# The opening of a decoder kernel: x normalised before its transposes, and even and odd modulation sums kept apart

## The reference

```python
def sandwich(x, fn, g_pre, g_post, shift, scale, gate, res_w):
    h = rms_norm(x, g_pre) * (1.0 + scale[:, None]) + shift[:, None]
    y = rms_norm(fn(h), g_post)
    return x + res_w * gate[:, None] * y
...
mod = cond @ ada_w[l] + ada_b[l]
sh1, sc1, gt1, sh2, sc2, gt2, sh3, sc3, gt3 = jnp.split(mod, N_MOD, axis=-1)
```

## Time and profile before

| | us |
|---|---|
| median of 3 runs | 1982.17 (1980.71 to 1982.24) |
| the profiled execution, its own time | 1987.39 |
| its span | 1985.6 |
| TensorE busy | 1886.3 |
| VectorE busy | 1412.9 |
| ScalarE busy | 838.1 |

### The profile page before, as it was taken

The page is one execution under the profiler, slowest core; times in us unless marked ns, Lnnn a source line. Parts: engine busy times, 40 slices in busy tenths (PEclk is TensorE's granted clock), DMA queues, the critical chain, the costliest instruction groups (busy, mean ns, idle before and its releaser), DMA issues.

```text
span 1985.6 us, 21419 instructions
## 1 busy us (share of the span) xinstructions
PE 1886.3 (95%) x8582; PEld 1546.5 (78%) x8582; DVE 1412.9 (71%) x1477; ACT 838.1 (42%) x1067; POOL 20.6 (1%) x25
## 2 busy tenths in 40 slices
PE   2779999999999998999999999999999999999997
PEld 2558888888888888777777787788888888888895
DVE  4987888888888887765765566666666665555556
ACT  2214434443444343374555534644344434443443
POOL 0000000000000000000000000000000000000000
PEclk6779999999999999999999999999999999999999
DMA  9888998999999998545333434566666655555551
GB/s 344 323 318 323 355 347 338 352 340 343 344 342 349 346 344 306 186 141 179 128 127 128 149 135 168 191 233 244 243 233 233 244 201 191 191 191 191 196 196 74
DMA packets 204002, 486.80 MB, mean 245 GB/s; under 512 B 7984, under 2 KB 20992, under 8 KB 188800
## 3 DMA queue, kind: packets, MB, share of 16 engines
q1 hardware_dynamic: 202816, 482.79, 67.1%
q10 hardware_dynamic: 992, 2.63, 0.4%
q0 software_dynamic: 96, 0.02, 0.0%
HBM read 483.31 MB, written 2.10 MB: 244 GB/s over the span
## 4 chain that ended last, share of the span: by engine, by line
PE 86%; DVE 6%; issue 2%; DMA 2%; ACT 1%; DVEq 0%; SPq 0%; POOLq 0%; POOL 0%; ACTq 0%
PE ps_u L1373 10%; PE ps_g L1373 10%; PE ps_u L1374 9%; PE ps_u L1375 9%; PE ps_g L1375 9%; PE ps_g L1374 9%; PE ps_t L1373 4%; PE ps_t L1374 4%; PE ps_t L1375 4%; PE ps_y L1373 4%; PE ps_y L1374 4%; PE ps_y L1375 4%; DVE arena L1136 3%; DMA ada_raw<-in_ada_w 2%; DVE w_lo L842 1%
## 5 line engine op out<-in xcount | busy, mean ns | idle before, releaser
L842 DVE TENSOR_TENSOR w_lo<-w_raw,w_hi 128x1024 fp32r<-128x1024 f32 (+1 forms) x632 | 753.1, 1200 | 458.4 <-ACT w_hi L505 457.2
L505 ACT ACTIVATE w_hi<-w_raw 128x1024 fp32r<-128x1024 f32 (+1 forms) x632 | 657.4, 1042 | 952.1 <-PE ps_u L1375 342.1
L1373 PE MATMUL ps_g<-w_hi,xT_hi 128*128 128x512 f32 (+1 forms) x880 | 347.1, 394 | 21.4 <-DVE w_lo L842 11.4
L1373 PE MATMUL ps_u<-w_hi,xT_hi 128*128 128x512 f32 (+2 forms) x880 | 348.0, 395 | 19.1 <-DVE w_lo L842 18.3
L1375 PE MATMUL ps_g<-w_hi,xT_lo 128*128 128x512 f32 (+1 forms) x880 | 341.8, 388 | 0.0
L1375 PE MATMUL ps_u<-w_hi,xT_lo 128*128 128x512 f32 (+2 forms) x880 | 341.8, 388 | 0.0
L1374 PE MATMUL ps_g<-w_lo,xT_hi 128*128 128x512 f32 (+1 forms) x880 | 341.6, 388 | 0.0
L1374 PE MATMUL ps_u<-w_lo,xT_hi 128*128 128x512 f32 (+2 forms) x880 | 341.5, 388 | 0.0
L866 DVE SCALAR_TENSOR_TENSOR arena<-ada_raw,cond,arena 128x2048 f32<-128x2048 f32 x108 | 253.6, 2348 | 32.7 <-DMA ada_raw<-in_ada_w 32.0
L1373 PEld LDWEIGHTS ps_g<-w_hi,xT_hi 128*128 128x128 f32 x880 | 166.3, 189 | 62.4 <-DVE w_lo L842 19.4
L1373 PEld LDWEIGHTS ps_u<-w_hi,xT_hi 128*128 128x128 f32 x880 | 167.1, 190 | 58.8 <-DVE w_lo L842 22.6
(11 more groups left out here) (239 smaller groups left out, 1542.5 us busy)
## 6 DMA issues: line engine op xcount, KB each, us to landing
w_raw<-in_ffn_w_in SPq DMA_DIRECT2D x160, 1024.0 KB, 4.9
ada_raw<-in_ada_w SPq DMA_DIRECT2D x128, 1024.0 KB, 7.2
w_raw<-in_ffn_w_out SPq DMA_DIRECT2D x80, 1024.0 KB, 5.1
w_raw<-in_mix_w_in SPq DMA_DIRECT2D x32, 1024.0 KB, 5.0
arena<-in_ada_w SPq DMA_DIRECT2D x16, 1024.0 KB, 10.2
w_raw<-in_mix_w_out SPq DMA_DIRECT2D x16, 1024.0 KB, 5.0
w_raw<-in_ffn_w_in SPq DMA_DIRECT2D x16, 768.0 KB, 4.6
w_raw<-in_ffn_w_out SPq DMA_DIRECT2D x8, 768.0 KB, 4.2
```

Of the source, the lines that this page charges most:

```text
L505: nc.scalar.activation(w_hi[:, u % 4, 0:n, 0:width], w_raw[:, s, 2 * hf:2 * hf + n, 0:width], ACT.Copy).then_inc(hi_done, 1)
L842: nc.vector.tensor_tensor(w_lo[:, u % 4, 0:n, 0:width], w_raw[:, s, 2 * hf:2 * hf + n, 0:width], w_hi[:, u % 4, 0:n, 0:width].bitcast(F32) ...
L1373: nc.tensor.matmul(o, a_hi[:, k, rows], w_hi[:, b, c, 0:width], start=start, stop=False)
```

## The change

- x is normalised before it is transposed. ScalarE takes the squares, GpSimd the power, and ScalarE multiplies x by 1/rms per token, into `yacc`. TensorE transposes that, 16 transposes for each token tile. The diagonal, the row `rbc`, `xt_scale` and the old `xt_hi` and `xt_lo` are gone. In a strip ScalarE applies scale and shift in one pass in place (two instructions of 256 columns for each pair of chunks) and rounds in a second (one of 512), and VectorE subtracts (one of 512).
- A tile of `ada_w` now holds two k-chunks of both modulations, loaded by two DMAs of 512 KB instead of one of 1 MB. VectorE handles both modulations with one instruction of 2 x 512 columns. Even k-chunks go into `acc`, odd ones into `junk`; there are 16 instructions in a strip. TensorE adds the two in PSUM: `first_sums` has 16 matmuls instead of eight.
- In strip s VectorE does the lo part of units 2 to 5, each followed by two tiles of strip s + 1, and then `strip_start(s + 1)`: it waits for the sums, forms the columns, makes units 0 and 1 of strip s + 1 and the xT rest of all four chunks. TensorE's order (units 0 to 3, sums, units 4 and 5) is as before. `first_xt_hi` stands behind unit 1 on ScalarE.
- c is loaded first and has its own transpose; 50 filler matmuls stand before the transposes of x and 40 before the first sums. Four small loads of constants move from ScalarE's queue to the end of the first SwiGLU on SyncE's, and the instruction on `sink` with them.

```diff
-ADA_PRE = 32
+STRIP_TILES = 8
+ADA_PRE = STRIPS * STRIP_TILES
 MODS_PRE = ((0, 1), (1, 2))
 
 
...
+def first_count(s, i):
+
+    return STRIP_TILES * s + i + 1
 
 
 def ada_total(mod):
...
         s_done, e_done, p_ready = sem("s_done"), sem("e_done"), sem("p_ready")
                 for i in range(LOOP):
                     hidden(i + 2, g0 + 5 + 3 * i, NB)
                 if f == 0:
+                    sp.dma_start(dist_a[:, :], consts[:, 128:512]).then_inc(const_landed, 16)
+                    sp.dma_start(dist_b[:, :], consts[:, 512:896]).then_inc(const_landed, 16)
+                    sp.dma_start(kvg[:, :], kvn_in[0:1, :].broadcast_to((P, KV_RANK))).then_inc(const_landed, 16)
+                    sp.dma_start(sink[:, :], sinks_in[0:1, :].broadcast_to((P, A_HEADS))).then_inc(const_landed, 16)
...
-            sp.dma_start(small_rows[4 * KD:6 * KD, :], ada_b[0, 0:2 * D].rearrange("(k p) -> k p", p=P)).then_inc(c_landed, 16)
-            sp.dma_start(small_rows[3 * KD:4 * KD, :], c_in[0].rearrange("(k p) -> k p", p=P)).then_inc(c_landed, 16)
+            sp.dma_start(mod_rows[:, :], c_in[0].rearrange("(k p) -> k p", p=P)).then_inc(cond_landed, 16)
             for n in range(3):
                 sp.dma_start(small_rows[n * KD:(n + 1) * KD, :], norm_g[0, 2 * n].rearrange("(k p) -> k p", p=P)).then_inc(c_landed, 16)
-            sp.dma_start(small_rows[6 * KD:8 * KD, :], ada_b[0, 3 * D:5 * D].rearrange("(k p) -> k p", p=P)).then_inc(c_landed, 16)
+            sp.dma_start(small_rows[3 * KD:5 * KD, :], ada_b[0, 0:2 * D].rearrange("(k p) -> k p", p=P)).then_inc(c_landed, 16)
+            sp.dma_start(small_rows[5 * KD:7 * KD, :], ada_b[0, 3 * D:5 * D].rearrange("(k p) -> k p", p=P)).then_inc(c_landed, 16)
             sp.dma_start(more_rows[:, :], ada_b[0, 6 * D:8 * D].rearrange("(k p) -> k p", p=P)).then_inc(c_landed, 16)
...
-                for a in range(8):
-                    kg, m = divmod(a, 2)
-                    count = 8 * s + a
-                    need(sp, ada_done, count - 3)
-                    sp.dma_start(first_slots[a % 4].rearrange("p (k n) -> p k n", n=NB),
-                                 ada_w[0].rearrange("(k p) n -> p k n", p=P)[:, 4 * kg:4 * kg + 4, m * D + s * NB:m * D + (s + 1) * NB]
-                                 ).then_inc(ada_landed[a % 4], 16)
+                for i in range(STRIP_TILES):
+                    before, j = (s, i - 4) if i >= 4 else (s - 1, i + 4)
+                    if before >= 0:
+                        sp.wait_ge(ada_done, first_count(before, j))
+                    for m in range(2):
+                        slot = first_slots[i % 4][:, m * 2 * NB:(m + 1) * 2 * NB].rearrange("p (k n) -> p k n", k=2)
+                        sp.dma_start(slot, ada_w[0].rearrange("(k p) n -> p k n", p=P)[:, 2 * i:2 * i + 2, m * D + s * NB:m * D + (s + 1) * NB]
+                                     ).then_inc(ada_landed[i % 4], 16)
...
-            act.dma_start(x_sb[:, :, :], x_in[0].rearrange("(t p) d -> p t d", p=P)).then_inc(x_landed, 16)
-            act.dma_start(dist_a[:, :], consts[:, 128:512]).then_inc(const_landed, 16)
-            act.dma_start(dist_b[:, :], consts[:, 512:896]).then_inc(const_landed, 16)
-            act.dma_start(kvg[:, :], kvn_in[0:1, :].broadcast_to((P, KV_RANK))).then_inc(const_landed, 16)
-            act.dma_start(sink[:, :], sinks_in[0:1, :].broadcast_to((P, A_HEADS))).then_inc(const_landed, 16)
+            for t in range(TILES):
+                act.dma_start(x_sb[:, t, :], x_in[0, t * P:(t + 1) * P, :]).then_inc(x_landed, 16)
+            act.wait_ge(cond_raw, 1)
+            nc.scalar.activation(cond[:, :], ps_y[:, 1, 0:KD], ACT.Silu).then_inc(cond_ready, 1)
             act.wait_ge(small_done, 1)
             nc.scalar.activation(gpre[:, :, :], ps_y[:, 0, 0:3 * KD].rearrange("p (n k) -> p n k", k=KD), ACT.Copy)
-            nc.scalar.activation(bias1[:, :, :], ps_y[:, 0, 4 * KD:10 * KD].rearrange("p (n k) -> p n k", k=KD), ACT.Copy)
-            nc.scalar.activation(cond[:, :], ps_y[:, 0, 3 * KD:4 * KD], ACT.Silu).then_inc(cond_ready, 1)
+            nc.scalar.activation(bias1[:, :, :], ps_y[:, 0, 3 * KD:9 * KD].rearrange("p (n k) -> p n k", k=KD), ACT.Copy).then_inc(cond_ready, 1)
...
-                    act.wait_ge(x_landed, 16)
-                    nc.scalar.activation(junk, x_sb[:, t, :], ACT.Square, accum_out=ss[:, 2 + t:3 + t]).then_inc(xsq_done, 1)
+                    act.wait_ge(x_landed, 16 * TILES)
+                    nc.scalar.activation(yacc[:, t, :], x_sb[:, t, :], ACT.Square, accum_out=ss[:, 2 + t:3 + t]).then_inc(xsq_done, 1)
...
+            def first_xt_hi(b):
+
+                act.wait_ge(modcol_done, b // 2 + 1)
+                for c in range(2):
+                    k = 2 * b + c
+                    ins = nc.scalar.activation(xT_raw[:, k, :], xT_raw[:, k, :], ACT.Identity, bias=modcol[:, 0, 1, k:k + 1],
+                                               scale=modcol[:, 0, 0, k:k + 1])
+                link(ins)
+                nc.scalar.activation(xT_hi[:, 2 * b:2 * b + 2, :], xT_raw[:, 2 * b:2 * b + 2, :], ACT.Copy).then_inc(xt_hi_done, 1)
...
+            first_x_squares()
+            act.wait_ge(rstd_ready, 1)
+            for t in range(TILES):
+                nc.scalar.activation(yacc[:, t, :], x_sb[:, t, :], ACT.Copy, scale=rstd[:, 2 + t:3 + t]).then_inc(xn_first, 1)
             for b in range(8):
-                act.wait_ge(xt_done, b + 1)
-                nc.scalar.activation(xT_raw[:, 2 * b:2 * b + 2, :], banks[b % 6].rearrange("p (c n) -> p c n", n=SEQ), ACT.Copy).then_inc(xt_copied, 1)
-                if b == 3:
-                    first_x_squares()
-            row_scale(0)
+                act.wait_ge(xt_done, b + 1 if b < 4 else 8)
+                nc.scalar.activation(xT_raw[:, 2 * b:2 * b + 2, :], banks[b].rearrange("p (c n) -> p c n", n=SEQ), ACT.Copy).then_inc(xt_copied, 1)
+            act.wait_ge(xt_copied, 8)
             for s in range(STRIPS):
-                if s == 0:
-                    xt_hi(0, 0)()
-                    xt_hi(0, 1)()
                 for i in range(2 * OPENING):
                     v = 2 * OPENING * s + i
                     hi_group(v // 8, 4, NB, None, range(v % 8, v % 8 + 1))
-                    if s + 1 < STRIPS and i >= 2 * OPENING - 2:
-                        xt_hi(0, 2 * s + i - 2)()
+                    if i == 1:
+                        first_xt_hi(2 * s)
+                        first_xt_hi(2 * s + 1)
...
+            def first_ada(s, i):
+
+                start = i == 0
+                dve.wait_ge(ada_landed[i % 4], 32 * (2 * s + i // 4) + 32)
+                for k in range(2):
+                    part = (acc[:, 1:3, s * NB:(s + 1) * NB], odd[:, s % 2, :, :])[k]
+                    raw = first_slots[i % 4].rearrange("p (m k n) -> p m k n", m=2, k=2)[:, :, k, :]
+                    weight = cond[:, 2 * i + k:2 * i + k + 1]
+                    if start:
                         ins = nc.vector.tensor_scalar(part, raw, weight, None, ALU.mult)
                     else:
+                        if k == 0:
+                            dve.wait_ge(dve_chain, evens[0])
+                        else:
+                            dve.wait_ge(ada_done, first_count(s, i) - 1)
                         ins = nc.vector.scalar_tensor_tensor(part, raw, weight, part, ALU.mult, ALU.add)
-                    if k == 3:
+                    if k == 1:
                         ins.then_inc(ada_done, 1)
                     else:
                         ins.then_inc(dve_chain, 1)
                         chain[0] += 1
-
-            def first_cols(s):
+                        evens[0] = chain[0]
+
+            def first_lo(v):
+                lo_group(v // 8, 4, NB, None, range(v % 8, v % 8 + 1))
+
...
+            def first_xt_lo(b):
+
+                dve.wait_ge(xt_hi_done, b + 1)
+                nc.vector.tensor_tensor(xT_lo[:, 2 * b:2 * b + 2, :], xT_raw[:, 2 * b:2 * b + 2, :],
+                                        xT_hi[:, 2 * b:2 * b + 2, :].bitcast(F32), ALU.subtract).then_inc(xt_lo_done, 1)
+
+            def strip_start(s):
+
+                first_columns(s)
+                first_lo(2 * OPENING * s)
+                first_lo(2 * OPENING * s + 1)
+                first_xt_lo(2 * s)
+                first_xt_lo(2 * s + 1)
+
+            dve.wait_ge(cond_ready, 1)
+            first_ada(0, 0)
+            dve.wait_ge(xsq_done, 2)
+            nc.vector.tensor_scalar(ss[:, 2:4], ss[:, 2:4], 1.0 / D, EPS, ALU.mult, ALU.add).then_inc(var_ready, 1)
+            norms[0] += 1
+            for i in range(1, STRIP_TILES):
+                first_ada(0, i)
+            dve.wait_ge(cond_ready, 2)
+            strip_start(0)
             for s in range(STRIPS):
-                for i in range(2 * OPENING):
+                for i in range(2, 2 * OPENING):
                     first_lo(2 * OPENING * s + i)
-                    if s + 1 < STRIPS and i < 4:
```

(65 more changed lines are left out.)

97 lines of the change are left out of this document (8 added, 89 removed).

## The result

| | before | after |
|---|---|---|
| median (lowest to highest), 7 runs each | 1982.17 (1980.71 to 1985.96) | 1991.41 (1987.13 to 1993.84) |
| profiled execution, its span | 1987.39, 1985.6 | 1992.49, 1990.7 |

The ratio after to before is 1.0038, with a 95% interval of 1.0027 to 1.0049: slower by 9.2 us, where the forecast had 5.3.

A forecast was written before the change was run, and what follows sets the result against it. VectorE's chain with TensorE's sums was taken to bound the opening, TensorE's own pace the rest. First mark -0.6, strips +5.8 and tail +0.1 gave +5.3 us on the median 1982.17: 1987.5 us, range 1977 to 1993.

The forecast's parts named there:

- The sums: 32 in 7.1 us at 1.2 GHz: TensorE's 32 sum instructions per strip, all on the path at the slow clock: 7.1 us, against 4.1 at 2.4 GHz.
- VectorE in a strip: Time between VectorE's first instructions behind successive sums: 34.5, 35.65 and 35.65 us, together 105.8 against 100.0, +5.8 us.
- Step 1: From a strip's mark until unit 2's lo part starts: 4.7 us in strip 0, 5.85 us from strip 1 on.
- Step 3: VectorE's 16 accumulation instructions of 1024 columns in a strip, mostly 1.20 us each: 18.2 us where before 20.7 stood.
- The first mark: -0.6 us: VectorE's first instruction behind the first sums, with TensorE's filler chain ending last: 45.9 us against 46.5.
- From the last mark on: +0.1 us: Last mark to the opening's end, eight TensorE units instead of seven and a half: 23.9 against 23.85 us.
- Costed at nothing: the constants: Four constant loads and the `sink` instruction, now late in the first SwiGLU: no TensorE wait on them, 0 us.
- The clock did not rise in the sums: Rival: clock rises during each strip's sums, which take 6.4 us; change -1.0 us, 1981 us; chance 0.16.
- it did not stay up: Rival: TensorE keeps 2.4 GHz up to the sums, 4.1 us each; about -9.5 us, 1972.7; chance 0.12.
- Longer instructions do save: Rival claimed the opposite: VectorE's 2 x 512 columns cost two times 0.66 us; 1993 us; chance 0.08.
- early-start rival: Start fillers all at 2.4 GHz: first mark 5 us earlier, 1982 us; chance 0.08.
- The halved loads were not slow: Rival claimed the opposite: eight more `ada_w` loads per strip cost 2.0 us each; some +35 us, 2020; chance 0.02.

The follow-up runs named there:

- after_fill_sums: Kernel after with 42 filler matmuls ahead of the sums of strips 1, 2 and 3: 1984.59 us, ratio to before 1.0001.
- after_sums_halved: Kernel after with VectorE adding odd sums to even ones, so TensorE has eight sum matmuls again: 1983.81 us, ratio to before 1.0002.
- after_no_start_fillers: Kernel after without the 50 and the 40 filler matmuls at the start: 1989.77 us, ratio to before 1.0033.
- after_short_ops: Kernel after with each accumulation instruction of 2 x 512 columns split into two of 512: 1997.67 us, ratio to before 1.0075.

## Why the prediction came out as it did

- **What bounds.** Right. VectorE's chain with TensorE's sums in it sets the end of the opening, and TensorE's own pace what follows.
- **The sums: 32 in 7.1 us at 1.2 GHz.** Right to the digit: 7.08 us, three times, PEclk 0.50. TensorE was idle for 10.2 to 11.2 us before them in the two profiles, against the 8 I worked out; at 0.50 either way, this changed nothing. Shown by after_fill_sums and after_sums_halved, which take away one factor each, the clock and the number, and each give back 7 to 8 us of the strips.
- **VectorE in a strip.** Right. Step 1 gave 4.7 us in strip 0 and 5.85 in strips 1 and 2; measured from mark to unit 2's lo part 4.85, 6.34 and 5.43. Step 3's 1.20 us was 1.20 us (four in 4.87). Distances of 34.5, 35.65 and 35.65 became 34.63, 36.12 and 35.21: 105.96 against 105.8.
- **The first mark: -0.6 us.** Mis-sized; it was -3.3. The first fillers took 13.37 us where I had 14.2. The second ones ran without a slow stretch (9.17 for 80, where I had 10.7): 2.7 us without a matmul did not bring the clock down here. The sums took 4.3 us, where I had 4.6. That the fillers would be the end of this chain was right, and after_no_start_fillers shows it.
- **From the last mark on: +0.1 us.** Right: 24.2 and 23.4 us in two profiles against 23.75 (the prediction had 23.85, with the end put at 170.4 us instead of 170.30).
- **Against which before.** This step failed. I took the strips of before as 100.0 us and put the difference on the median. But this profile was 5.2 us above its median, and a part of the excess lay in the very part that I compared: two slow sums in three. The mean of three profiles is 98.9 us, so the strips lost 7.3 us on average. Most of the excess lay behind the opening: the first SwiGLU, up to the fillers before the token mixer, took 669.9 us in this profile and 665.1 and 665.0 us in the two others. With the first mark at -3.2 (43.5 against 46.7) and nothing at the tail, the opening's end moved by +4.1 us.
- **Costed at nothing: the constants.** This term was wrong at nothing. I had written that TensorE has no wait on these loads. It has none on the loads themselves, but the tile of `ada_w` behind them lands later, VectorE waits for it, and TensorE waits for VectorE: 1.1 and 1.7 us in the two profiles of after. Behind the opening the profiles give 1813.2 us for before (three) and 1816.1 for after (two), +2.9; over all runs, 1814.0 for the seven with early constants and 1816.0 for the seven with late ones. The difference lies in the first SwiGLU, which took 667.4 us on average with early constants (665.0 to 669.9) and 670.1 with late ones (667.7 to 671.8). TensorE's idle time in its last 125 us was 6.5 and 9.3 us. Of these 2.7 us the wait shown accounts for 1.9 on average; the rest is not traced, and the ranges overlap. The fourteen profiles are of different kernels, but each of the three pairs that differ in the constants alone has TensorE's wait on one side only. From the fillers on, every profile took either some 1145.4 or some 1147.1 us, each in seven profiles and both in either kernel; why is not known, but the change has no part in it. With +4.1 and +2.9 the profiles sum to 7.0 us, where the two comparisons of medians gave 9.2 and 6.4.
- **The rivals.** The clock did not rise in the sums (0.50 throughout), and it did not stay up. Longer instructions do save (after_short_ops, +7.6 us without them). The first mark was earlier by 2.6 us than forecast, about half of the early-start rival. The halved loads were not slow: behind the first tile VectorE waited 0.2 to 1.0 us for each tile (two loads) at the start and in the strips not at all, with 384 to 408 GB/s in the windows. The Trainium skill's rule ("DMA: Bandwidth & Descriptors", section "Rules for kernel authors": 1 MiB or more per DMA) did not bind for pairs of 512 KB issued back to back; that speaks of this case alone.
- **The number.** 1987.5 was 3.9 us low, inside the range, and the side was the likeliest one. It came as near as that partly by luck. The baseline's profile (1.5 us) and what came behind the opening (2.9 us, of it some 1.4 by the wait behind the constants) were missing on one side and the first mark (2.6 us) on the other, so that behind 5.3 forecast and 7.0 in the profiles stand three terms that were off by 1.5 to 2.9 us in both directions. The 2.2 us between those 7.0 and the 9.2 of the medians are explained by no profile.

## What to carry to other kernels

Where two engines wait for each other at a joint, price TensorE's work there by the slower clock unless it comes to it busy. Here a small TensorE task behind an idle time of 10 us took 7.1 us where full speed would have needed some 4 (the first sums took 4.3). It is better halved on the other engine or preceded by fillers, but only in time that is idle in every iteration, the last one too. A few small loads moved out of the way can stand in the way elsewhere: look at which load is issued right behind them and who waits for it. Before a difference is worked out from one profile, ask which of its durations differ from one execution to the next, and take a second profile of the same kernel: the marks of a stage, read across several, tell more than one median. A chain that an edit takes off one engine may have had another, such as the fillers, right behind it.
